# Two latent norms: squares taken together, column sums, reciprocals and scalings placed later

## The reference, cut to what matters

```python
u = rms_norm_2(h, norm_mix)
z, xbc, dt_raw, q_a, c_kv, k_rope, gate_ssd, gate_mla = split_cols(u @ w_in, IN_SPLITS)
y_ssd = ssd_branch(z, xbc, dt_raw, ...) @ w_ssd_out     # conv4 + silu on xbc, scan in 4 groups
# latent branch: q_a is 384 wide, c_kv is 256 wide
q  = rms_norm_2(q_a,  q_a_norm)  @ w_q_b
kv = rms_norm_2(c_kv, kv_a_norm) @ w_kv_b
# rms_norm_2(x, g) = x * rsqrt(mean(x*x) + eps) * g
```

## Time and profile before

| | |
|---|---|
| median of 3 executions | 1463.07 us (1462.75 to 1463.22) |
| the profiled execution | 1462.93 us, its span 1461.1 us |
| busy share of the span | PE 93%, PEld 84%, DVE 70%, ACT 57%, POOL 5% |
| the chain that ended last | PE 78%, DVE 13%, ACT 5%, issue 2%, DMA 1%, POOL 1% |
| granted clock of TensorE, mean | 0.976 of full speed |

### The profile page before, as it was taken

How to read it: one execution, slowest core, us unless ns; L and a number is a source line. 1 busy time by engine, 2 the same in 40 slices (tenths; PEclk the granted TensorE clock), 3 DMA queues, 4 the chain that set the end, 5 groups by cost and what they waited for, 6 DMA issues and landing times.

```text
span 1461.1 us, 23661 instructions
## 1 busy us (share of the span) xinstructions
PE 1366.0 (93%) x9387; PEld 1230.9 (84%) x9390; DVE 1023.0 (70%) x1522; ACT 835.7 (57%) x1209; POOL 77.8 (5%) x64
## 2 busy tenths in 40 slices
PE   6999999997999998899999999999997899999994
PEld 5888999996999996789998777799995677777773
DVE  6666555556555556798777654576457999999994
ACT  4245544454444444566554422365546899999993
POOL 0000100000000000000001000012000011111113
PEclk9999999998999999899999999999998999999997
DMA  7544465552465542545433422456452899999973
GB/s 249 174 126 138 149 199 173 184 190 87 149 195 177 199 138 69 159 148 173 145 120 110 154 81 93 144 174 192 155 200 94 352 355 355 356 366 370 352 272 117
DMA packets 149020, 278.75 MB, mean 191 GB/s; under 512 B 13401, under 2 KB 121790, under 8 KB 135486
## 3 DMA queue, kind: packets, MB, share of 16 engines
q1 hardware_dynamic: 142158, 271.15, 53.7%
q0 software_dynamic: 6768, 6.31, 1.4%
HBM read 274.28 MB, written 21.50 MB: 202 GB/s over the span
## 4 chain that ended last, share of the span: by engine, by line
PE 78%; DVE 13%; ACT 5%; issue 2%; DMA 1%; POOL 1%; DVEq 0%; ACTq 0%; POOLq 0%; SPq 0%
PE psum L833 17%; PE psum L835 17%; PE psum L834 17%; PE psum L1371 3%; PE psum L1372 3%; PE psum L1373 3%; PE psum L956 2%; PE psum L1396 2%; DVE weights_parts L2436 2%; DVE weights_parts L1930 2%; PE psum L1398 2%; PE psum L1397 2%; DVE arena L2278 1%; PE psum L873 1%; PE psum L797 1%
## 5 line engine op out<-in xcount | busy, mean ns | idle before, releaser
L1930 DVE TENSOR_TENSOR weights_parts<-ring,weights_parts 128x1024 fp32r<-128x1024 f32 (+1 forms) x284 | 341.7, 1219 | 214.5 <-ACT weights_parts L1433 214.1
L833 PE MATMUL psum<-xnorm_parts,weights_parts 128*128 128x256 f32 (+2 forms) x1536 | 443.5, 289 | 22.0 <-DVE xnorm_parts L1945 15.9
L834 PE MATMUL psum<-xnorm_parts,weights_parts 128*128 128x256 f32 (+2 forms) x1536 | 435.5, 284 | 0.0
L835 PE MATMUL psum<-xnorm_parts,weights_parts 128*128 128x256 f32 (+2 forms) x1536 | 435.1, 283 | 0.0
L1433 ACT ACTIVATE weights_parts<-ring 128x1024 fp32r<-128x1024 f32 (+1 forms) x284 | 292.1, 1045 | 219.9 <-PE psum L835 219.9
L833 PEld LDWEIGHTS psum<-xnorm_parts,weights_parts 128*128 128x128 f32 (+2 forms) x1536 | 289.4, 188 | 39.5 <-issue 28.9
L834 PEld LDWEIGHTS psum<-xnorm_parts,weights_parts 128*128 128x128 f32 (+2 forms) x1536 | 289.8, 189 | 1.4 <-issue 1.0
L835 PEld LDWEIGHTS psum<-xnorm_parts,weights_parts 128*128 128x128 f32 (+2 forms) x1536 | 289.6, 189 | 0.3
L834 PE MATMUL psum<-hidden_parts,weights_parts 128*128 128x256 f32 x512 | 143.8, 281 | 0.0
L833 PE MATMUL psum<-hidden_parts,weights_parts 128*128 128x256 f32 x512 | 143.8, 281 | 0.0
L835 PE MATMUL psum<-hidden_parts,weights_parts 128*128 128x256 f32 x512 | 143.8, 281 | 0.0
(11 more groups left out here) (381 smaller groups left out, 2441.2 us busy)
## 6 DMA issues: line engine op xcount, KB each, us to landing
expert_raw<-in_w_exp_down SPq DMA_DIRECT2D x35, 1024.0 KB, 7.5
ring<-in_mlp_w_up SPq DMA_DIRECT2D x32, 1024.0 KB, 5.4
ring<-in_mlp_w_down SPq DMA_DIRECT2D x32, 1024.0 KB, 4.8
ring<-in_w_in SPq DMA_DIRECT2D x30, 1024.0 KB, 5.3
ring<-in_w_exp_gate SPq DMA_DIRECT2D x23, 1024.0 KB
ring<-in_w_exp_up SPq DMA_DIRECT2D x23, 1024.0 KB
ring<-in_attn_w_qkv SPq DMA_DIRECT2D x12, 1024.0 KB, 5.5
expert_raw<-in_w_exp_gate SPq DMA_DIRECT2D x12, 1024.0 KB
```

What stands on the lines that cost most here:

```text
L833: pe.matmul(out, lh, rh, start=start, stop=False, **more)
L834: pe.matmul(out, lh, rl, start=False, stop=False, **more)
L835: return pe.matmul(out, ll, rh, start=False, stop=stop, **more)
L1930: dve.tensor_tensor(low, src, high.bitcast(F32), ALU.subtract).then_inc(s["lo_ready"], 1)
```

## The change

In turn j = 1 ScalarE takes only the squares, of norm 6 and right behind them of norm 7, whose squares now lie in tiles 3 and 4 of `sq`. TensorE makes both column sums after chunk j = 4. ScalarE takes both roots at the end of its turn j = 5, into `std[:, 1]` and `std[:, 2]`. VectorE's reciprocal and scaling of norm 6 stand in state-space group 0, those of norm 7 in group 1, after the sixteen `m_ready` instructions and ahead of the last two `feed(2)`. The number of matmuls, activations, reciprocals and scalings is the same.

```diff
@@ TensorE, xbc loop
-                if j == 1:
+                if j == 4:
                     norm_sum(6)
-                    norm_sum(7)
+                    norm_sum(7, sq[:, 3:5, :])
@@ ScalarE, squares(n)
-                    act.activation(sq[:, k0:k1, :], src[:, k0:k1, :], ACT.Square).then_inc(s["sq_ready"], 1)
+                    first = 3 if n == 7 else 0
+                    act.activation(sq[:, first + k0:first + k1, :], src[:, k0:k1, :],
+                                   ACT.Square).then_inc(s["sq_ready"], 1)
@@ ScalarE, xbc loop
                 if j == 1:
-                    norm(6)
-                    norm(7)
+                    squares(6)
+                    squares(7)
+                if j == 5:
+                    act.wait_ge(s["xn_ready"], XN_NO[6])
+                    for n in (6, 7):
+                        b = wait_full("norm", n)
+                        act.activation(std[:, n - 5, :], bank(b)[:, 0:TOK], ACT.Sqrt, bias=eps_col[:, 0:1],
+                                       scale=1.0 / (NORM[n][1] * P)).then_inc(made[b], 1)
@@ VectorE, new
+            def latent_norm(n):
+
+                src, tiles, gain, first, dst, _ = NORM[n]
+                inverse = std[:, n - 5, :]
+                wait_made("norm", n)
+                link(dve.reciprocal(inverse, inverse))
+                for k in range(tiles):
+                    dve.scalar_tensor_tensor(dst[:, k, :], src[:, k, :], col(gain, first + k), inverse,
                                              ALU.mult, ALU.mult).then_inc(s["xn_ready"], 1)
@@ VectorE, in each group, behind the loop that signals m_ready
                     ins.then_inc(s["m_ready"], 1)
+                if g < 2:
+                    latent_norm(6 + g)
                 feed(2)
```

More of the change, by code:

```diff
@@ L2339, in ssd_norm @@
                                              ALU.mult, ALU.mult).then_inc(s["xn_ready"], 1)
+            def latent_norm(n):
[5 more added lines that the diff above has]
+                    dve.scalar_tensor_tensor(dst[:, k, :], src[:, k, :], col(gain, first + k), inverse,
+                                             ALU.mult, ALU.mult).then_inc(s["xn_ready"], 1)
             wait_made("dtT", 0)
```

## The result

| kernel | median of the runs | lowest to highest | profiled: time, span |
|---|---|---|---|
| before | 1463.12 us (4 runs) | 1462.75 to 1463.22 | 1462.93, 1461.1 |
| changed | 1450.93 us (4 runs) | 1450.50 to 1453.27 | 1450.61, 1448.8 |

The ratio is 0.992, with a 95% interval of 0.9904 to 0.9935. The forecast was 1452.3 us, its range 1450.2 to 1455.8. All nine runs of the changed kernel have their median at 1452.47.

The account below looks back on a forecast made before the run. TensorE paces most stages but stood idle at the norms in turn 1, with VectorE pacing turns 2 to 7; 11.1 us gained at `conv(2)` less 0.4 in group scalings gives 10.7, so 1452.3 us, range 1450.2 to 1455.8.

Parts of the forecast that it names:

- The start of `conv(2)`: VectorE in the xbc loop: third convolution starts at 601.3 instead of 612.44, 11.1 us earlier.
- The distance from `conv(2)` to the end: Sign over the rest of the kernel: prediction wrong if this differs from before by more than 1.5 us.
- The sums after chunk 4: TensorE, xbc loop: ten sums, 2.2 us, make chunk 5 0.8 us late; hidden by VectorE's work, no cost.
- The waits for VectorE: Sign on TensorE in the xbc loop: waits of some 0.7 us remain from chunk 6 on.
- The roots in turn 5: ScalarE, xbc loop: next half about 1 us later, within a 4.7 us cushion; no cost, 3.5 us if uncovered.
- The drain: ScalarE, table loads: by the skill's 1.38 us each, roots would cost 2.8 us more, still inside the 4.7 us cushion.
- The scalings in the groups: VectorE, groups 0 and 1: 3.0 and 2.6 us, mostly hidden behind TensorE; cost 0.4 us, bounds zero and 5.6.
- The sum: Whole kernel: 11.1 less 0.4 gives a gain of 10.7 us, forecast 1452.3 us.
- The clock: TensorE behind the change: shifted slow stretches add or take 1 us, counted in the range, not the sum.
- A: Rival, groups 0 and 1: scalings don't hide, up to 5.6 us instead of 0.4, 1457.5 us; chance 0.13, part or whole.
- B: Rival, xbc loop: VectorE's queue sets it, sums and roots cost 2.2 + 3.5 us more, 1458.0 us; chance 0.04.
- C: Rival, groups: late z chunk half idles TensorE, clock falls, kernel slower, 1469.6 us; chance 0.02 with similar cases.

Follow-up runs that it names:

- e7b_five_more: Changed kernel with five more sum matmuls (ten rows, 2.2 us, results unused) ahead of the sums behind chunk 4; run once, 1453.84 us.
- e7_sums_twice: Changed kernel with ten more sum matmuls (twenty rows, 4.3 us, results unused) ahead of the sums behind chunk 4; median 1453.74 us.
- e3_sums_late: Changed kernel with the column sums behind chunk 9 instead of 4 and the roots in turn 10 instead of 5; median 1453.69 us.
- e5_norm6_ahead: Changed kernel with the scaling of norm 6 moved ahead of group 0; median 1451.01 us.
- e8_both_early: Changed kernel with softplus part 0 ahead of the xbc loop, parts 1 to 5 in turns 1 to 5, norm 6's scaling ahead of group 0; median 1449.31 us.
- e2_scalings_in_loop: Changed kernel with reciprocals and scalings in turns 5 and 6 of the xbc loop instead of the groups; median 1458.31 us, ratio to before 0.9961.
- e1_squares_first: Kernel before with only both norms' squares taken together; sums, roots and scalings stay in turn 1; median 1462.9 us, ratio 0.9995.

## Why the prediction was right

**The start of `conv(2)`.** Predicted 11.1 us earlier, at 601.3; it was 601.50 with the trace starting 0.35 us later, so 11.3. The way there, squares, half, low part, was as told, each within 0.2 us. To measure the gain where VectorE takes over, rather than by TensorE's idle time, was the step that mattered: 4.83 + 1.18 us of idle time and 4.9 of sums make 10.9, close by chance, while chunk 2's end alone would have given 11.7. The distance from `conv(2)` to the end, which was not to differ from that of before by more than 1.5 us, is 1.4 us shorter in the first profile and 0.7 longer in the second: within the bound, and near it only by the stretch between D and E.

**The sums after chunk 4.** Predicted: no cost, chunk 5 is 0.8 us late with a cushion. Confirmed by e7b_five_more (no cost at 3.0 us of lateness), e7_sums_twice (2.2 us at 5.1) and e3_sums_late (2.0 us where there is no cover). The waits for VectorE do not remain from chunk 6 on, as I wrote, but from chunk 7 on: chunk 6 found its bank just free.

**The roots in turn 5.** Predicted: no cost, the next half about 1 us later. ScalarE's timeline of the changed kernel, and VectorE's taking up that half:

```profile
620.51 1.06 ACT L1433 ACTIVATE weights_parts<-ring 128x1024 fp32r<-128x1024 f32 x1
621.58 1.28 ACT L1664 ACT_TABLE_LOAD   x1
622.88 0.84 ACT L1664 ACTIVATE std<-psum,eps_col 128x256 f32<-128x256 f32 x2
623.61 1.06 ACT L1433 ACTIVATE weights_parts<-ring 128x1024 fp32r<-128x1024 f32 x1
```

```profile
627.78 1.23 DVE L1938 TENSOR_TENSOR weights_parts<-ring,weights_parts 128x1024 fp32r<-128x1024 f32 x1
```

The half ends at 624.7, 3.1 us ahead of its use; it was 4.7 before. Its delay is 1.6 us rather than 1. The table load at 621.58 begins where the half at 620.51 ends, and the roots begin 0.02 us behind the load. The drain that the Trainium skill ("ScalarE: Activation LUTs", "What ACT_TABLE_LOAD costs") puts beside each load, which the prediction weighed, doesn't show here either. No run takes the roots alone away, so their cost of nothing is read from the timeline, not tested.

**The scalings in the groups.** Predicted 0.4 us between zero and 5.6, at the second of the two banks that `decay` frees in group 1. B to C is 0.5 us longer, the chain goes through just these instructions, and the wait is at the third row of line 1088. e5_norm6_ahead takes the wait away but only 0.2 us of the distance, e8_both_early all of it. That the lag ends in group 1 held too: the idle time ahead of the last `feed(2)` shrank from 3.52 to 1.25 us and didn't vanish.

**The sum.** 11.3 less 0.5 is 10.8 where 10.7 was predicted; both terms are a little larger than their forecasts (11.1 and 0.4), and they offset each other in part. The mechanism thus held. That a median of a few executions lands so near 1452.3 is in part luck, for the reason that follows.

**The clock, the term that was too small.** I took 1 us either way for the slow stretches behind the change. The one between D and E moved D to E by 1.6 to 2.1 us, and another between C' and D is worth some 1.6 us. The nine executions of the changed kernel lie 3.9 us apart (1450.50 to 1454.37); how much of that is the clock's is not shown, as two of them were profiled, and the mean clock over the whole span doesn't put them in order (1450.50 us at 0.978, 1453.27 at 0.980). The Trainium skill, "TensorE: Matmul & The Clock Gate", has it in its part on the clock gate that the same kernel can have a different number of slow matmuls from run to run; the two profiles of the changed kernel agree, with 30.3 and 32.4 us for the same work. The first four runs lay on the lower side of the forecast by 1.4 us, the later five above it by 1.4.

**The rivals.** A (nothing hides in the groups) would have shown up to 5.6 us in B to C; it was 0.5. B (given back in the loop) would have shown in A to B; e2_scalings_in_loop shows that VectorE's queue does set the loop, but the gain passes through it, as every turn starts earlier. C (slower) needed TensorE to idle at a z chunk in group 1; it didn't.

## What to carry to other kernels

When one engine idles and another takes over the pace right behind, read a gain from the start of the instruction of the second engine that the chain enters next, and follow the two or three instructions that lead to it. A side chain that nobody needs soon (here a norm whose result is read a hundred microseconds later) belongs in each engine's queue where another engine sets the pace: its matmuls where VectorE does, its vector work where TensorE does; the same 5.6 us of work cost 0.5 in one place and 5.6 in the other. Compare variants by distances between the same instructions of two traces, as effects below 2 us vanish in the medians.

## What the hardware showed that I had not expected

The slow stretches of TensorE's clock are worth 1.3 to 2.1 us each and their length can differ between executions of one kernel: D to E is 30.3 or 32.4 us in two of them. C' to D is 264.4, 266 or 267.6 us for the same instructions in different kernels. Whether a shift of the work moves them as well is not shown. Ahead of A, in stages that no edit touches, the profiled executions differ by 6.3 us; of the 3.6 us by which e3_sums_late is late at A, 2.0 are there at 330 us and all at 350, and how much of that is the clock's is not shown. A few executions can look sharper than the kernel is: the kernel before had 1462.75 to 1463.22 us in four of them, and 1462.19 to 1468.02 in fourteen.

The half clock also cost more at the old place than the idle time. In e1_squares_first the removal of a wait of 1.18 us brought 2.1 us, as the clock rose earlier (0.72 against 0.60 from 597 to 609 us).

And in e2_scalings_in_loop TensorE's wait of 3.63 us for VectorE was followed by a first product of 0.58 us instead of 0.39 and a stretch at 1.2 GHz in a loop that had none (a mean of 0.97 from 600 to 650 us); the waits of 0.64 us in the changed kernel left the clock at full speed.

```profile
600.00:650.00 50.00, 44.06 (x346) 43.03 (x345) 48.20 (x80) 31.19 (x45) 0.00 (x0) 0.97 0.44 141
```
